# Values stationary and scaled probabilities moving for head pairs, in a two-block attention kernel

## The chip, the cores and the metric

One core of a Trainium2 chip runs the whole kernel. The metric is the device time of one execution in microseconds (us).

## The reference

Two transformer blocks work on one sequence of 256 tokens, width 1024, head width 64, all in f32. The first block has two layers; each runs four kinds of attention side by side (neighbourhood, differential, grouped-query, latent; 4 heads of each, the differential ones with two probability matrices). The second block has four layers: sliding-window, gated linear, forgetting, sliding-window. A feed-forward part follows every attention. Per head the attention is

```
p = softmax(q @ k.T * scale + table)      # 256 x 256, some heads causal, sliding heads with a sink in the sum
o = p @ v                                 # 256 x 64
```

and the heads side by side (256 x 1024) go through w_o.

## The kernel before

Weights come in units of 1 MB. ACT casts each to its leading part (`whi`, L885), DVE subtracts to get the rest (`wlo`, L894, sometimes in halves), and PE multiplies with three products of leading parts and rests. PE does a unit in four quarters.

A `Plan` says for each slot of a layer which quarters PE does, at which slot a head begins (`begin`), when a turn is made and which half units DVE splits. There are four plans: MIX (first block, 20 heads, of which 0 to 7 are the differential ones, called pair heads here, and 12 plain), SWA and FOX (sliding, forgetting, 16 plain causal heads each), and GLA (no heads of this kind). If head k begins in slot h, its steps are these.

- Slot h: PE computes the scores into a bank of `psu` (L751). DVE adds the table and finds the negated maximum (L846), or only the maximum (L840). ACT takes the exponential with its sums (L810, for a sink L808 before it) into `prob` and raises `p_ready`.
- Slot h+2: PE waits for `p_ready` and transposes `prob` into `pso` (L737), three 128x128 blocks for a causal head, four for another. ACT copies them to `probT` (L796).
- Slot h+3: PE multiplies `probT` (stationary, 128x128) by the values (64 columns moving) into `psm` (L766). DVE adds the sink to the sum (L819), takes the reciprocal (L821) and multiplies into `rows` (L828).
- "Turns": when the 128 columns m of the output (two heads) are in `rows`, PE transposes them into `psu` bank 1 (L612), ACT casts them to `ahi` (L645) and DVE subtracts to get `alo` (L649). These are the stationaries of w_o, whose quarters (the slab, L632) fill the last slots.

"Joint" pairs have both scores computed in one slot, side by side on the two halves of the partitions; the second head's go to bank 2 of `psy`, which the slab later takes, so that pairs are joint only up to the slot `pairs_to`.

Each engine runs its queue in order. In one slot DVE's is: maximum of the head that begins, division of the head three slots back, turn, rotary embedding (L1559 to L1563, SWA alone), half unit of `wlo`, and for two slots of the first SWA layer a modulation reduction (L1096). In a few slots the division comes first. ACT's is: copy of the transposed probabilities, exponential, casts of outputs, turn, `whi`.

## Time and profile before

| | |
|---|---|
| median of 3 runs | 1897.2 us (1896.7 to 1898.39) |
| profiled execution | 1897.12 us |
| its span | 1895.1 us |
| granted clock, mean | 0.998 |
| PE, DVE, ACT busy | 1855.8, 1354.9, 953.2 us |

The span runs from the first to the last instruction of the core. A timeline row starts with the start in us and the busy time in us. Matmuls overlap in the pipeline, so the pace of PE is read from start to start, not from busy times. L12 is line 12 of the kernel; names before the arrow are what is written. In brackets stands idle time ahead of the row and what ended it.

### The profile page before, as it was taken

The page shows a single profiled execution, that of the slowest core. Times are in us where ns is not written, and L with a number is a line of the kernel's source. Part 1 is how long each engine was busy: PE and PEld are TensorE (multiplying, and loading weights), DVE is VectorE, ACT ScalarE, POOL GpSimd, SP SyncE. Part 2 cuts the span into 40 slices and gives each one's busy share as a digit, 9 for nine tenths or more (in the row PEclk, how much of TensorE's full clock was granted, in tenths as well). Part 3 has the DMA queues.
Part 4 walks back from the last instruction along what each step waited for, and adds up shares of the span by engine and source line. Part 5 has one row for each costly group of instructions (what it writes and reads, how often), then busy time and mean ns, then how long its engine had stood idle before and what let it go on. Part 6 is the DMA issues. An engine that isn't in the chain of part 4 may idle for free.

```text
span 1895.1 us, 34211 instructions
## 1 busy us (share of the span) xinstructions
PE 1855.8 (98%) x13368; PEld 1702.6 (90%) x13368; DVE 1354.9 (71%) x2194; ACT 953.2 (50%) x1470; POOL 77.0 (4%) x98
## 2 busy tenths in 40 slices
PE   8999999999999999999999999999999999999998
PEld 8989999998999987899989799998989998979997
DVE  6758888775878877888877587886555556766555
ACT  7755334766533466533473553345654334664333
POOL 3003000000000000000000000003300000000000
PEclk9999999999999999999999999999999999999999
DMA  8538987533788742788854388875335554335552
GB/s 305 188 125 259 353 307 304 190 134 134 290 329 307 297 177 97 262 326 308 315 198 139 119 300 323 306 279 225 122 138 190 192 181 165 132 113 199 189 187 89
DMA packets 62060, 416.60 MB, mean 220 GB/s; under 512 B 9008, under 2 KB 9200, under 8 KB 13312
## 3 DMA queue, kind: packets, MB, share of 16 engines
q1 hardware_dynamic: 56016, 401.33, 57.4%
q0 software_dynamic: 5936, 13.79, 2.6%
q8 instruction: 72, 1.18, 0.2%
q14 instruction: 36, 0.29, 0.0%
HBM read 413.90 MB, written 3.19 MB: 220 GB/s over the span
## 4 chain that ended last, share of the span: by engine, by line
PE 89%; DVE 6%; ACT 2%; issue 1%; DVEq 1%; ACTq 0%; DMA 0%; SPq 0%
PE psu L524 35%; PE psy L692 18%; PE psy L586 7%; PE psy L578 5%; PE psy L632 5%; PE psu L541 4%; PE psm L766 3%; PE psy L565 2%; PE psu L751 2%; PE pso L737 1%; PE psy L655 1%; DVE x L1164 1%; DVE wlo L894 1%; PE psy L1680 1%; DVEq L1163 1%
## 5 line engine op out<-in xcount | busy, mean ns | idle before, releaser
L885 ACT CAST whi<-raw 128x2048 fp32r<-128x2048 f32 (+1 forms) x281 | 536.2, 1908 | 599.1 <-PE psu L524 396.4
L894 DVE TENSOR_TENSOR wlo<-raw,whi 128x2048 fp32r<-128x2048 f32 (+5 forms) x306 | 646.6, 2114 | 257.2 <-ACT whi L885 256.5
L524 PE MATMUL psu<-hlo,whi 128*128 128x256 f32 x1920 | 536.0, 279 | 0.0
L524 PE MATMUL psu<-hhi,whi 128*128 128x256 f32 x1920 | 535.9, 279 | 0.0
L524 PE MATMUL psu<-hhi,wlo 128*128 128x256 f32 x1920 | 535.8, 279 | 0.0
L524 PEld LDWEIGHTS psu<-hhi,whi 128*128 128x128 f32 x1920 | 360.8, 188 | 2.3
L524 PEld LDWEIGHTS psu<-hlo,whi 128*128 128x128 f32 x1920 | 360.8, 188 | 2.3
L524 PEld LDWEIGHTS psu<-hhi,wlo 128*128 128x128 f32 x1920 | 360.8, 188 | 0.0
L1096 DVE CUSTOM_DVE_ANT_0 ada_raw<-ada_raw,cvec 128x1024 f32<-128x1024 f32 x192 | 227.0, 1220 | 2.2 <-DMA ada_raw<-ada 2.2
L692 PE MATMUL psy<-whi,ahi 128*128 128x512 f32 x528 | 210.2, 398 | 0.0
L692 PE MATMUL psy<-wlo,ahi 128*128 128x512 f32 x528 | 207.9, 394 | 0.0
L692 PE MATMUL psy<-whi,alo 128*128 128x512 f32 x528 | 207.4, 393 | 0.0
L586 PE MATMUL psy<-whi,hhi 128*128 128x256 f32 x448 | 131.4, 293 | 0.0
L586 PE MATMUL psy<-wlo,hhi 128*128 128x256 f32 x448 | 125.9, 281 | 0.0
L586 PE MATMUL psy<-whi,hlo 128*128 128x256 f32 x448 | 125.8, 281 | 0.0
L692 PEld LDWEIGHTS psy<-wlo,ahi 128*128 128x128 f32 x528 | 99.1, 188 | 25.4
L692 PEld LDWEIGHTS psy<-whi,alo 128*128 128x128 f32 x528 | 99.1, 188 | 21.0
L692 PEld LDWEIGHTS psy<-whi,ahi 128*128 128x128 f32 x528 | 99.1, 188 | 20.5
L586 PEld LDWEIGHTS psy<-whi,hhi 128*128 128x128 f32 x448 | 84.5, 189 | 4.9 <-issue 4.8
L766 PEld LDWEIGHTS psm<-work 128*128 128x128 f32 x608 | 76.1, 191 | 13.5 <-issue 7.2
L810 ACT ACTIVATE work<-work,nmax 128x256 f32<-128x256 f32 (+1 forms) x144 | 66.5, 463 | 40.9 <-DVE nmax L846 40.9
L586 PEld LDWEIGHTS psy<-whi,hlo 128*128 128x128 f32 x448 | 84.6, 189 | 0.1
(337 smaller groups left out, 2981.2 us busy)
## 6 DMA issues: line engine op xcount, KB each, us to landing
raw<-wts SPq DMA_DIRECT2D x280, 1024.0 KB, 4.8
ada_raw<-ada SPq DMA_DIRECT2D x96, 1024.0 KB, 5.0
gain<-gate_rows POOLq DMA_DIRECT2D x8, 512.0 KB, 3.9
dense_bias<-rel_bias POOLq DMA_DIRECT2D x32, 64.0 KB, 10.1
nab<-dense_bias SPq DMA_DIRECT2D x2, 1024.0 KB, 7.1
ada_raw<-fox_rows POOLq DMA_DIRECT2D x4, 512.0 KB, 13.3
cb<-cst POOLq DMA_DIRECT2D x1, 1408.0 KB, 8.2
cb<-cst SPq DMA_DIRECT2D x1, 1056.0 KB, 10.1
```

What stands on the lines that cost most here:

```text
L524: last = mm(psu[:, bank, cc * SEQ:(cc + 1) * SEQ], a[:, cols], h[:, kt, :], start=(kt == 0 and j == 0), stop=(kt == KT - 1 and j == 2))
L541: last = mm(psu[:, banks[u], cc * SEQ:(cc + 1) * SEQ], a[:, cols], h[:, kt, :], start=(kt == 0 and cc == 0 and j == 0), stop=(kt == KT - 1 ...
L565: last = mm(psy[:, j, half * width:(half + 1) * width], h[:, kt, toks], a[:, kt * width:(kt + 1) * width], start=start, stop=stop, skip_gr ...
L578: last = mm(o, a[:, cols], h[:, kt, :], start=(kt == 0 and j == 0), stop=(kt == KT - 1 and j == 2))
L586: last = mm(o, h[:, kt, toks], a[:, kt * width:(kt + 1) * width], start=(kt == 0 and j == 0), stop=(kt == KT - 1 and j == 2))
L632: last = mm(psy[:, 2 * t + half, :], h[:, (2 * s + ff) % 4, toks], b[:, cols], start=(s == 0 and ff == 0 and j == 0), stop=(s == 3 and ff ...
L692: last = mm(psy[:, 2 * t + half, :], h[:, aslot + ff, toks], b[:, cols], start=(first_step and ff == 0 and j == 0), stop=(last_step and ff ...
L766: last = mm(psm[:, t * HD:(t + 1) * HD], probT[:, k % 2, at:at + P], it["v"][kc], start=(kc == 0), stop=(kc == 1 or at == P))
L810: last = nc.scalar.activation(prob[:, k % 2, span], src[:, span], ACT.Exp, bias=nmax[:, k % 4, t:t + 1], scale=1.0 if plain else -1.0, acc ...
L885: nc.scalar.copy(whi[:, part_of(c), 0:n], raw[:, slot_of(c), 0:n]).then_inc(hi_done, 1)
L894: last = nc.vector.tensor_tensor(wlo[:, part_of(c), cols], raw[:, slot_of(c), cols], whi[:, part_of(c), cols].bitcast(f32), ALU.subtract)
L1096: last = nc.vector.tensor_tensor_reduce(tile, tile, cvec[:], 1.0, 0.0, ALU.mult, ALU.add, ada_part[:, 2 * half + j:2 * half + j + 1])
```

## The change

1. For plain heads the product with the values is made for two heads at once, in the odd head's slot: values stationary (128x64), `probT` moving (256 columns, or 128 for the causal half), the even head into partitions 0 to 63 of `psm`, the odd one into 64 to 127. The output comes out transposed, and the PE turn falls away, but for the two of MIX that hold pair heads and the eight of GLA. ACT and DVE make `ahi` and `alo` from SBUF.
2. The normalisation goes ahead of the transposition: DVE's `dve_roots` (sink added, reciprocal) stands first in the slot after the scores, and waits for `p_ready`; ACT's `act_normal` scales `prob` in place before that slot's exponential. PE's transposition waits for it (`pn_ready`).
3. The division of two heads becomes one copy of 128x256 from `psm` (L865 of the changed kernel).
4. `probT` has three buffers, not two.
5. In SWA and FOX the second head's scores go to bank 1 of `psu`, which no turn uses now. `pairs_to` rises from 23 to 25 in FOX and from 16 to 20 in SWA: five more pairs are joint (two in each SWA layer, one in FOX). Two waits of the slab for `max_ready` go.

The diff, cut:

```diff
    [14, 16, 18, 20, 26, 27, 28, 30], "00 10 01 11 02 12 03 13",
-   [2, 3] + [2 * j + 1 for j in range(2, 11)] + [24, 25, 27, 29, 31, 33], 23)
+   [2, 3] + [2 * j + 1 for j in range(2, 11)] + [24, 25, 27, 29, 31, 33], 25)
 SWA = Plan([4] * 6, [2] * 8 + [1] * 15 + [2, 2, 1, 2, 2], range(6, 22), [11, 13, 15, 17, 20, 21, 23, 25],
-   "00 01 10 02 03 11 12 13", [2, 4, 6, 8, 13, 17, 20, 24], 16)
+   "00 01 10 02 03 11 12 13", [2, 4, 6, 8, 13, 17, 20, 24], 20)
 GLA = Plan([4] * 13, [3, 4, 1] + [1] * 60, [], [45, 46, 49, 50, 52, 53, 55, 57], "00 10 01 11 02 12 03 13",
...
-prob, probT = fold(w(8000, 1024), 2, 512), fold(w(9024, 1024), 2, 512)
+prob, probT = fold(w(8000, 1024), 2, 512), fold(w(9024, 1536), 3, 512)
...
-def act_turn(act, l, c, m, g, bank=1):
...
-    act.wait_ge(m_tr, 8 * g + m + 1)
+def act_turn(act, l, c, m, g, src, *ready):
+    act.wait_ge(*ready)
...
-    nc.scalar.copy(ahi[:, m % 4], psu[:, bank, 0:SEQ]).then_inc(m_hi, 1)
...
-def dve_turn(dve, m, g, bank=1):
+    nc.scalar.copy(ahi[:, m % 4], src).then_inc(m_hi, 1)
+def dve_turn(dve, m, g, src):
...
-    nc.vector.tensor_tensor(alo[:, m % 4], psu[:, bank, 0:SEQ], ahi[:, m % 4].bitcast(f32), ALU.subtract).then_inc(m_lo, 1)
+    nc.vector.tensor_tensor(alo[:, m % 4], src, ahi[:, m % 4].bitcast(f32), ALU.subtract).then_inc(m_lo, 1)
 def pe_norm(pe, m, q, idle=0, ahead=4):
...
 def score_at(plan, k):
-    return psy[:, 2] if plan.joint[k] and k % 2 == 1 else psu[:, 0]
+    second = psy[:, 2] if plan is MIX else psu[:, 1]
+    return second if plan.joint[k] and k % 2 == 1 else psu[:, 0]
 def spans(it):
...
+def turned_at(it, t, kc, at):
+    return at if it["causal"] or it["pair"] is not None else kc * SEQ + t * P
+def columns(plan, m):
+    at = 256 if plan is MIX and m == 4 else m * SEQ
+    return scratch[:, at:at + SEQ]
+def plain_no(I0, items, k):
+    before = sum(it["pair"] is None for it in items[:k])
+    return I0 - 8 * min(I0 // 20, DEPTH1) + before
 def pe_begin(pe, I0, items, plan, h):
...
-        pe.wait_ge(p_ready, I0 + k + 1)
+        if items[k]["pair"] is None:
+            pe.wait_ge(pn_ready, plain_no(I0, items, k) + 1)
+        else:
+            pe.wait_ge(p_ready, I0 + k + 1)
...
-        for _, _, at in blocks(items[k]):
-            last = nc.tensor.transpose(pso[:, at:at + P], prob[:, k % 2, at:at + P], ident[:])
+        for t, kc, at in blocks(items[k]):
+            to = turned_at(items[k], t, kc, at)
+            last = nc.tensor.transpose(pso[:, to:to + P], prob[:, k % 2, at:at + P], ident[:])
...
         it = items[k]
+        if it["pair"] is None and k % 2 == 0:
+            return
         pe.wait_ge(pt_ready, I0 + k + 1)
         if k >= 1:
-            pe.wait_ge(o_evac, I0 + k)
+            pe.wait_ge(o_evac, I0 + k - (it["pair"] is None))
         if it["vpre"] is not None:
             pe.wait_ge(*it["vpre"])
+        if it["pair"] is None:
+            for kc in range(2):
+                for i in (k - 1, k):
+                    toks, at = (slice(kc * P, SEQ), P + kc * SEQ) if it["causal"] else (slice(0, SEQ), kc * SEQ)
+                    last = mm(psm[HD * (i % 2):HD * (i % 2) + HD, toks], items[i]["v"][kc],
+                              probT[:, i % 3, at:at + toks.stop - toks.start], start=(kc == 0), stop=(kc == 1))
+            last.then_inc(o_done, 2)
+            return
         for t, kc, at in blocks(it):
-            last = mm(psm[:, t * HD:(t + 1) * HD], probT[:, k % 2, at:at + P],
+            last = mm(psm[:, t * HD:(t + 1) * HD], probT[:, k % 3, at:at + P],
                       it["v"][kc], start=(kc == 0), stop=(kc == 1 or at == P))
...
-def pe_mix_turn(pe, I0, plan, h, g):
...
-    m = plan.turn.get(h)
-    if m is not None:
-        pe.wait_ge(o_evac, I0 + 2 * m + 2)
-        pe_turn(pe, g, m)
...
 def pe_mix1_turn(pe, l, I0, h):
     m = MIX.turn.get(h)
-    if m is not None:
-        if m < 2:
-            pe.wait_ge(mix_ready, l + 1)
-        else:
-            pe.wait_ge(o_evac, I0 + 2 * m + 6)
+    if m is not None and m < 2:
+        pe.wait_ge(mix_ready, l + 1)
         pe_turn(pe, l, m)
 def act_copy(act, I0, items, plan, h):
...
         act.wait_ge(t_done, I0 + k + 1)
-        if k >= 2:
-            act.wait_ge(o_done, I0 + k - 1)
+        if k >= 3:
+            act.wait_ge(o_done, I0 + k - 2)
         lo = spans(items[k])[0].start
-        nc.scalar.copy(probT[:, k % 2, lo:], pso[:, lo:]).then_inc(pt_ready, 1)
+        nc.scalar.copy(probT[:, k % 3, lo:], pso[:, lo:]).then_inc(pt_ready, 1)
 def act_exp(act, I0, items, plan, h):
...
-def dve_divide(dve, I0, it, k):
+def act_normal(act, I0, items, plan, h):
+    k = plan.score(h - 1)
+    if k is not None and items[k]["pair"] is None:
+        act.wait_ge(r_ready, plain_no(I0, items, k) + 1)
+        for t, span in enumerate(spans(items[k])):
+            last = nc.scalar.activation(prob[:, k % 2, span], prob[:, k % 2, span], ACT.Copy, scale=rsum[:, k % 4, t:t + 1])
+        last.then_inc(pn_ready, 1)
+def dve_roots(dve, I0, items, plan, h):
+    k = plan.score(h - 1)
+    if k is not None and items[k]["pair"] is None:
+        dve.wait_ge(p_ready, I0 + k + 1)
+        if items[k]["sink"] is not None:
+            nc.vector.tensor_tensor(psum_[:, k % 4], psum_[:, k % 4], esink[:, k % 4], ALU.add)
+            nc.vector.drain()
+        nc.vector.reciprocal(rsum[:, k % 4], psum_[:, k % 4]).then_inc(r_ready, 1)
+def dve_divide(dve, I0, items, plan, k):
+    it = items[k]
+    if it["pair"] is None:
+        if k % 2 == 1:
+            dve.wait_ge(o_done, I0 + k + 1)
+            m = k // 2 - (2 if plan is MIX else 0)
+            nc.vector.tensor_copy(columns(plan, m), psm[:, 0:SEQ]).then_inc(o_evac, 2)
+        return
     dve.wait_ge(o_done, I0 + k + 1)
-    if it["sink"] is not None:
-        nc.vector.tensor_tensor(psum_[:, k % 4], psum_[:, k % 4], esink[:, k % 4], ALU.add)
-        nc.vector.drain()
     nc.vector.reciprocal(rsum[:, k % 4], psum_[:, k % 4])
...
 def dve_steps(dve, I0, items, plan, h, g, divide_first=False):
+    dve_roots(dve, I0, items, plan, h)
...
-        dve_divide(dve, I0, items[k], k)
+        dve_divide(dve, I0, items, plan, k)
...
     if k is not None and not divide_first:
-        dve_divide(dve, I0, items[k], k)
+        dve_divide(dve, I0, items, plan, k)
     if second is not None:
...
     if h in plan.turn:
-        dve_turn(dve, plan.turn[h], g)
+        m = plan.turn[h]
+        dve_turn(dve, m, g, psu[:, 1, 0:SEQ] if plan is MIX and m < 2 else columns(plan, m))
...
                     pe.wait_ge(swa_evac, s5 + (4 if part == 0 else 5))
-                    if part == 2:
-                        pe.wait_ge(max_ready, I0 + sum(SWA.joint))
                 pe_slab_quarter(pe, DEPTH1, c0 + 6, j - 6, part, g)
...
                     pe.wait_ge(bank_free, b0 + (12 if part == 0 else 13))
-                    if part == 0:
-                        pe.wait_ge(max_ready, I0 + sum(FOX.joint))
                 pe_slab_quarter(pe, DEPTH1, c0 + 13, j - 13, part, g, 1 if j == 13 else 0)
...
         pe_value(pe, I0, items, FOX, h)
-        pe_mix_turn(pe, I0, FOX, h, g)
         if h == 4:
...
+        act_normal(act, I0, items, SWA, h)
...
         if h in SWA.turn:
-            act_turn(act, DEPTH1, c0 + 6, SWA.turn[h], g)
+            m = SWA.turn[h]
+            act_turn(act, DEPTH1, c0 + 6, m, g, columns(SWA, m), o_evac, I0 + 2 * m + 2)
         if h == 23:
...
```

MIX and FOX take the lines of ACT like SWA. Three places follow where the instructions move. DVE, plain slots of an SWA layer; L846 before is L894 after, L894 before is L944 after, `psum_` the sums. Before:

```order
L846 ISA work,nmax<-psu,cb,nsink 128x128 [waits t_done,s_done]
L846 ISA nmax 128x1
L846 ISA work,nmax<-psu,cb,nsink 128x256
L846 ISA nmax 128x1
L819 TENSOR_TENSOR psum_<-psum_,esink 128x2 [waits o_done]
L821 RECIPROCAL rsum<-psum_ 128x2
L828 TENSOR_TENSOR rows<-psm,rsum 128x2x64
L894 TENSOR_TENSOR wlo<-raw,whi 128x1024 [waits hi_done]
```

After:

```order
L854 TENSOR_TENSOR psum_<-psum_,esink 128x2 [waits p_ready]
L856 RECIPROCAL rsum<-psum_ 128x2
L894 ISA work,nmax<-psu,cb,nsink 128x128 [waits t_done,s_done]
L894 ISA nmax 128x1
L894 ISA work,nmax<-psu,cb,nsink 128x256
L894 ISA nmax 128x1
L865 COPY rows<-psm 128x256 [waits o_done]
L944 TENSOR_TENSOR wlo<-raw,whi 128x1024 [waits hi_done]
L854 TENSOR_TENSOR psum_<-psum_,esink 128x2 [waits p_ready]
```

The sum and the reciprocal went from behind the maximum, where they waited for PE, to ahead of it, where they wait for ACT's exponential. ACT, the same layer, before:

```order
L796 COPY work<-pso 128x384 [waits o_done,t_done]
L808 ACTIVATE esink<-nmax,prow 128x2 [waits max_ready]
L810 ACTIVATE work,psum_<-work,nmax 128x128
L810 ACTIVATE work,psum_<-work,nmax 128x256
L645 CAST ahi<-psu 128x256 [waits m_tr]
```

After:

```order
L818 COPY work<-pso 128x384 [waits o_done,t_done]
L844 ACTIVATE work<-work,rsum 128x128 [waits r_ready]
L844 ACTIVATE work<-work,rsum 128x256
L830 ACTIVATE esink<-nmax,prow 128x2 [waits max_ready]
L832 ACTIVATE work,psum_<-work,nmax 128x128
L832 ACTIVATE work,psum_<-work,nmax 128x256
L647 CAST ahi<-rows 128x256 [waits o_evac]
```

Two scalings, with a wait for DVE, stand now between copy and exponential. PE, two slots of an SWA layer (an odd head with its turn), before:

```order
L751 MATMUL psu<-work 128x128 [waits swa_evac,max_ready]
L751 MATMUL psu<-work 128x256
L766 MATMUL psm<-work 128x64 [waits o_evac,pt_ready]
L766 MATMUL psm<-work 128x64 x2
L612 MATMUL psu<-ident,rows 128x128 [waits m_lo,o_evac]
L612 MATMUL psu<-ident,rows 128x128
```

After:

```order
L760 MATMUL pso<-ident,work 128x128 [waits pt_ready,pn_ready]
L760 MATMUL pso<-ident,work 128x128 x2
L774 MATMUL psu<-work 128x128 [waits swa_evac,max_ready]
L774 MATMUL psu<-work 128x128
L774 MATMUL psu<-work 128x256 x2
L794 MATMUL psm<-work 64x256 [waits o_evac,pt_ready]
L794 MATMUL psm<-work 64x256
L794 MATMUL psm<-work 64x128 x2
```

The value product is four instructions for two heads, the pair of scores is joint, and the turn is gone.

## Rows read from the trace of the kernel before

**Rows 1.** The page: busy time and instructions of each engine; its chain by engine.

```profile
PE 1855.8 (98%) x13368; PEld 1702.6 (90%) x13368; DVE 1354.9 (71%) x2194; ACT 953.2 (50%) x1470; POOL 77.0 (4%) x98
...
PE 89%; DVE 6%; ACT 2%; issue 1%; DVEq 1%; ACTq 0%; DMA 0%; SPq 0%
```

**Rows 2.** Windows: stretch, length, busy (instructions) of PE, PEld, DVE, ACT, POOL; clock, DMA.

```profile
712.00:726.00 14.00, 13.73 (x111) 12.05 (x110) 10.27 (x37) 9.65 (x32) 0.00 (x0) 1.00 0.05 7
1356.00:1372.00 16.00, 16.00 (x141) 15.50 (x141) 8.18 (x22) 9.76 (x22) 0.00 (x0) 1.00 0.39 133
116.00:132.00 16.00, 16.00 (x104) 14.09 (x104) 7.92 (x18) 9.78 (x24) 0.00 (x0) 1.00 0.34 133
```

**Rows 3.** Timeline of PE, sliding layer: start, busy, line, tiles, count.

```profile
704.52 0.78 PE L766 MATMUL psm<-work 128*128 128x64 f32 x6
705.11 0.36 PE L586 MATMUL psy<-whi,hhi 128*128 128x256 f32 x1
...
707.05 0.37 PE L751 MATMUL psu<-work 64*128 64x128 f32 x1
...
707.90 0.55 PE L766 MATMUL psm<-work 128*128 128x64 f32 x3
...
734.32 0.88 PE L766 MATMUL psm<-work 128*128 128x64 f32 x6
735.01 0.47 PE L632 MATMUL psy<-whi,ahi 128*128 128x512 f32 x1
```

**Rows 4.** Timeline of PE, first-block layer.

```profile
132.69 1.00 PE L766 MATMUL psm<-work 128*128 128x64 f32 x8
133.50 0.48 PE L632 MATMUL psy<-whi,ahi 128*128 128x512 f32 x1
133.82 0.40 PE L632 MATMUL psy<-whi,alo 128*128 128x512 f32 x1
134.06 0.39 PE L632 MATMUL psy<-wlo,ahi 128*128 128x512 f32 x1
...
136.39 0.38 PE L612 MATMUL psu<-ident,rows 128*128 128x128 f32 x2
136.53 0.48 PE L632 MATMUL psy<-whi,ahi 128*128 128x512 f32 x1
```

**Rows 5.** Timeline of PE, gated layer, a stationary of 64 columns.

```profile
1045.13 1.94 PE L1713 MATMUL psu<-work 128*64 128x256 f32 x8
```

**Rows 6.** Timeline of DVE, first sliding layer.

```profile
710.74 0.35 DVE L846 CUSTOM_DVE_ANT_0 work<-psy,cb,nsink 128x128 f32<-128x128 f32 x1 [1.15 <-PE pso L737]
...
711.42 0.16 DVE L819 TENSOR_TENSOR psum_<-psum_,esink 128x2 f32<-128x2 f32 x1
...
713.00 0.42 DVE L649 TENSOR_TENSOR alo<-psu,ahi 128x256 fp32r<-128x256 f32 x1 [0.82 <-ACT ahi L645]
...
715.64 0.15 DVE L819 TENSOR_TENSOR psum_<-psum_,esink 128x2 f32<-128x2 f32 x1
...
720.82 1.22 DVE L894 TENSOR_TENSOR wlo<-raw,whi 128x1024 fp32r<-128x1024 f32 x1
```

**Rows 7.** Timeline of ACT, first sliding layer.

```profile
711.54 0.29 ACT L808 ACTIVATE esink<-nmax,prow 128x2 f32<-128x2 f32 x1 [0.27 <-DVE nmax L846]
711.74 0.39 ACT L810 ACTIVATE work<-work,nmax 128x128 f32<-128x128 f32 x1
...
712.53 0.19 ACT L810 ACTIVATION_READ_ACCUMULATOR work<-work,nmax 128x1 f32 x1
712.62 0.35 ACT L645 CAST ahi<-psu 128x256 fp32r<-128x256 f32 x1
```

**Rows 8.** Timelines, PE of first, DVE and PE of second sliding layer.

```profile
750.62 0.49 PE L737 MATMUL pso<-ident,work 128*128 128x128 f32 x3
...
1644.14 0.35 DVE L846 CUSTOM_DVE_ANT_0 work<-psy,cb,nsink 128x128 f32<-128x128 f32 x1 [1.15 <-PE pso L737]
...
1682.97 0.49 PE L737 MATMUL pso<-ident,work 128*128 128x128 f32 x3
```

More of the change, by code:

```diff
@@ L260, in build @@
         o_evac = sem("o_evac")
+        r_ready = sem("r_ready")
+        pn_ready = sem("pn_ready")
         mix_ready = sem("mix_ready")
@@ L607, in pe_turn @@
         def pe_turn(pe, g, m, bank=1):
-            if not isinstance(m, int) or m > 0:
+            if m > 0:
                 pe.wait_ge(m_lo, 8 * g + m)
@@ L1329, in act_mix1 @@
                 act_copy(act, I0, items, MIX, h)
+                act_normal(act, I0, items, MIX, h)
                 act_exp(act, I0, items, MIX, h)
@@ L1374, in act_mix1 @@
                 if h in MIX.turn:
-                    act_turn(act, l, C1_O, MIX.turn[h], l)
+                    m = MIX.turn[h]
+                    if m < 2:
+                        act_turn(act, l, C1_O, m, l, psu[:, 1, 0:SEQ], m_tr, 2 * l + m + 1)
+                    else:
+                        act_turn(act, l, C1_O, m, l, columns(MIX, m), o_evac, I0 + 2 * m + 6)
                 if h == 33:
@@ L1599, in pe_swa @@
                     heads(SWA_HEADS[h])
-                pe_mix_turn(pe, I0, SWA, h, g)
         def pe_fox(pe, n, c0, b0):
@@ L1775, in act_fox @@
                 act_copy(act, I0, items, FOX, h)
+                act_normal(act, I0, items, FOX, h)
                 act_exp(act, I0, items, FOX, h)
@@ L1788, in act_fox @@
                 if h in FOX.turn:
-                    act_turn(act, DEPTH1, c0 + 13, FOX.turn[h], g)
+                    m = FOX.turn[h]
+                    act_turn(act, DEPTH1, c0 + 13, m, g, columns(FOX, m), o_evac, I0 + 2 * m + 2)
                 if h == 28:
@@ L1883, in act_gla @@
                 if h in GLA.turn:
-                    act_turn(act, DEPTH1, c0 + 13, GLA.turn[h], g, 0)
+                    act_turn(act, DEPTH1, c0 + 13, GLA.turn[h], g, psu[:, 0, 0:SEQ], m_tr, 2 * DEPTH1 + GLA.turn[h] + 1)
                 if h == 57:
@@ L1990, in dve_gla @@
                 if h in GLA.turn:
-                    dve_turn(dve, GLA.turn[h], g, 0)
+                    dve_turn(dve, GLA.turn[h], g, psu[:, 0, 0:SEQ])
                 if h in (4, 40):
```

## Prediction

> **What bounds the kernel now.** The first view is the page. PE is busy for 98% of the span and holds 89% of the chain; DVE holds 6%, ACT 2% [rows 1]. So what PE is spared shortens the kernel, as long as PE gets its inputs in time. Whether it does is not to be read from the means, so the second view is busy time by stretch [rows 2]. Among forgetting and first-block heads PE is busy for 16.00 of 16 us, with DVE at about 8 and ACT at 9.8: PE is the bound and the others have slack. Among sliding heads PE has 13.73 of 14 us, DVE 10.27, ACT 9.65. These heads have one quarter per slot, the ropes and the short slots, and the other engines wait for each other there. The third view is the timelines, for the prices and for the ring of waits between DVE and ACT.
>
> **PE, the part that is removed.** Heads of the sliding layer: six passes of a 64-column product take 704.52 to 705.11, 0.59 us; behind scores 734.32 to 735.01, 0.69 [rows 3]. Two heads: 1.28, and the change of format behind a product is paid once more (0.08: the first 512-column step behind it takes 133.50 to 133.82, 0.32, the next 0.24 [rows 4]). The new product of a pair has the passes of a joint pair of scores, two of 256 and two of 128 columns on each of two halves of the array. That pair takes 707.05 to 707.90, 0.85 [rows 3]. I take this for the values too: 1.36 - 0.85 = 0.51 saved per pair, 24 such pairs (16 sliding, 8 forgetting). A first-block head takes 132.69 to 133.50, 0.81 [rows 4], two of them with the change behind 1.70. The new pair has two passes of 256 where the causal pair has 128, so 0.85 + 2 x 0.12 = 1.09, with 0.24 per pass of 256 from 1.94 / 8 [rows 5]; 0.61 saved, 12 pairs.
>
> What no row shows is two *column* halves at once: rows 3 show two row halves of the array doing so. The bounds are 0.85 (they run side by side) and 0.85 + 0.72 = 1.57 (the second head's 256 + 256 + 128 + 128 columns behind the first's, three passes of 0.24, as the eight of rows 5 follow each other on one half). I take the lower end since the row that is nearest in form, two 64-wide tiles side by side, is the joint pair. The upper end is a rival. The Trainium skill, "TensorEngine Tiling (Array Packing)", Key Properties, says that tiles operate independently, but also "Mode switching requires drain". By its second rule each of the 36 products now drains the array twice, which the old ones with the whole array did not; the joint pair's 0.85, which begins with 128x128 transposes before it and a full-width product behind it, holds such a switch already, so the sum stays.
>
> Turns: 136.39 to 136.53, 0.14 [rows 4], and up to 0.22 with the step behind it; I take 0.18. There are eight turns in each of six layers; 12 of the 16 in MIX, 16 in SWA and 8 in FOX go, 36. Joint scores: a single head's scores take as long as a pair's, so 0.85 for each of five pairs. PE is spared 24 x 0.51 + 12 x 0.61 + 36 x 0.18 + 5 x 0.85 = 12.2 + 7.3 + 6.5 + 4.3 = **30.3 us**, if it never waits more.
>
> **DVE** loses the multiplication of each head (about 0.3) and gains a copy per pair (about 0.3): nothing to count. Its turn from SBUF is not dearer than the 0.42 us of now [rows 6].
>
> **ACT** gains two scalings for each of 72 heads. No row shows this; the nearest are the exponentials of the same blocks, 711.74 to 712.62, less two readings of the sum at 0.09 [rows 7]: 0.70 for a causal head, and with two of 256 columns 0.8. 48 x 0.70 + 24 x 0.8 = 53 us, of which nothing shows where ACT has its 6 us of slack in 16, as in the forgetting stretch.
>
> **The new ring.** Before, DVE could take the maximum of the next head while ACT was still at the exponential of this one. Now the sum and reciprocal stand ahead of that maximum and wait for the exponential. Everything DVE has queued ahead (turn, rope, half unit) then stands between this exponential and the next. One plain slot: roots 0.35; from the start of the maximum to ACT's start 710.74 to 711.54, 0.80; from there to the end of the exponential 1.08, and 0.12 for the signal (711.42 to 711.54). 2.35 us; the scaling (0.70) fits beside the 0.80. From the maximum of head 5 to that of head 15 in the first sliding layer: ten such, 23.5; five turns, each 713.00 - 711.54 + 0.42 - 1.20 = 0.68, 3.4; two ropes, each 715.64 - 713.00 - 0.42 = 2.2, 4.4; five half units at 1.22, 6.1; two modulation halves at 1.22, 2.4 [rows 6, 7]. Sum 39.8. To the transposition of head 15, which opens the rest of the slab: 0.80 + 1.20, a turn 0.68, a half 1.22, roots 0.35, scaling and signal 0.82, sum 5.1. So 44.9, where now 710.74 to 750.62 is 39.9 [rows 6, 8]: 5.0 later, less about 0.6 of product and turns that are cheaper behind it: **+4.4**. The second sliding layer has no modulation: 42.5, against 1644.14 to 1682.97, 38.8 [rows 8]: +3.7 - 0.6 = **+3.1**. PE's savings in front of the transposition are turned into waiting there.
>
> In the forgetting layer there is no rope, two quarters per slot keep PE at 16.00 of 16, and the ring has time: 8 x 0.51 + 8 x 0.18 + 0.85 = 6.4 saved, less 1 for the first heads, which wait behind a whole unit of DVE: **-5.4**. In the first block 6 x 0.61 + 6 x 0.18 = 4.8 per layer could be had. Some four heads begin in the 16 us, so ACT there goes from 9.8 to 9.8 + 4.2 x 0.8 = 13.2 [rows 2], and masks, turns and whole units of 2 us stand in DVE's queue ahead of roots. I give one third: **-1.6** per layer, between nothing and 4.8. Moving the banks of the scores takes no more than their waits; I cost it at nothing, as PE is behind its producers there.
>
> Sum: 4.4 + 3.1 - 5.4 - 3.2 = **-1.1 us**, from the profiled 1897.12 (the median is 1897.2, so it makes no difference): **1896.0 us**. A measurement of this kernel tells 0.2%, 3.8 us, from no change.
>
> **The rivals.**
>
> *A, the forecast: the ring bounds the sliding layers, tiles run side by side.* For it: the waits just worked out, and the 13.73 of 14. Against: my walk adds latencies in a row, and 1 us in ten slots on either side is easily missed. Own range 1889 to 1901. Chance 0.45.
>
> *B, column halves run one behind the other.* Place: the new product. Price: 0.72 more per causal pair, 0.96 per first-block pair. Against A: forgetting +5.8; first block: 6 x (0.96 - 0.61) - 6 x 0.18 = +1.0 and the delay of its first plain heads, 0.5, so 1.5 instead of -1.6, +6.2 for two layers; sliding +0.5 at most, as PE waits there. 1896.0 + 12.5 = 1908.5. It decides the sign from about 0.3 us more per pair. For it: every row with a 64-column stationary (rows 5) goes at one pass after the other. Against: the row halves do not. Chance 0.2. The Trainium skill, "TensorE: Matmul & The Clock Gate", Measured speedup vs the span model, gives 2.38x for three column tiles at once; by that page B falls, and no row of before shows it.
>
> *C, PE stays the bound everywhere.* DVE's and ACT's slack takes ring and scaling. 1897.1 - 30.3 = 1866.8; with the sliding ring as in A and the first block whole, 7.5 - 6.4 - 9.6 = -8.5, 1888.6. For it: the chain's 89% on PE. Against: ACT would have to do 0.70 more per slot of 3.6 us (39.9 / 11) in sliding layers and DVE never to stand behind it. Chance 0.25 for what lies from 1866 to 1889.
>
> *D, a dearer ring.* The half units that stand ahead of the roots themselves wait for ACT's cast to `whi`, which comes after its exponential, so that one late cast delays a whole slot. 2 us per layer more in three layers and the first block's third lost: 1896 + 6 + 3.2 = 1905. Chance 0.1.
>
> **How the numbers follow.** The time is A's. The range 1877 to 1909 takes in A, B and D and the dearer half of C; some 0.13 lies below, some 0.07 above. Faster by over 0.2% (under 1893.4): C with 0.25 and 0.12 of A, 0.37. Within: A's rest, 0.33, and 0.02 of D, 0.35. Slower: B and the rest of D, 0.28.
>
> **What would show it.** In the changed profile the value product should take 0.85 from start to start in sliding and 1.09 in first-block layers; 1.5 and more is B. The scaling should take 0.35 per instruction. In the sliding layers PE's transposition should wait for ACT's scaling, ACT for DVE's maximum, DVE's sum for ACT's exponential, and from the maximum of head 5 to the transposition of head 15 should be 45 us; with 40 or less A is wrong and C holds. In the forgetting layer PE should stay at 16 of 16. DVE's share of the chain should rise above its 6%. I would be most wrong if the transpositions of the first-block layers found the scaling ready each time.

## The result: 1908.1 us, 0.57% slower, and the profile after

| | before | after |
|---|---|---|
| median, 5 runs each | 1897.2 us (1896.7 to 1898.39) | 1908.1 us (1907.59 to 1909.43) |
| ratio | | 1.0057, 95% interval 1.0043 to 1.0072 |
| profiled execution, span | 1897.12, 1895.1 us | 1907.82, 1906.0 us |

Five runs of before, not three, stand behind 1897.2. The forecast was 1896.0, no change that could be told. The kernel is slower, clear of its interval; the time lies in the range of 1877 to 1909, near its upper end. The page after, against [rows 1]:

```profile
PE 1836.4 (96%) x13104; PEld 1658.1 (87%) x13104; DVE 1345.6 (71%) x2158; ACT 1005.9 (53%) x1614; POOL 78.1 (4%) x98
...
PE 84%; DVE 7%; ACT 5%; issue 2%; DVEq 2%; ACTq 1%; DMA 0%; SPq 0%
```

PE is busy 19.4 us less and holds 84% of the chain instead of 89%, and the kernel is 11 us longer. ACT is busy 52.7 us more; 53 was worked out. DVE and ACT have gained chain. The same three stretches of time as in [rows 2]; the work in them has moved by 2 to 11 us, so they show how full each engine is and not the same instructions:

```profile
712.00:726.00 14.00, 12.52 (x102) 10.00 (x101) 8.74 (x34) 12.31 (x38) 0.00 (x0) 1.00 0.21 75
1356.00:1372.00 16.00, 15.95 (x135) 14.01 (x135) 7.91 (x26) 13.12 (x33) 0.00 (x0) 1.00 0.38 132
116.00:132.00 16.00, 14.46 (x77) 10.31 (x76) 7.16 (x15) 11.65 (x31) 0.00 (x0) 1.00 0.23 78
```

The forgetting stretch is still full, 15.95 of 16. In the sliding and first-block stretches PE now stands still for 1.5 us each. In the sliding one ACT is nearly as busy as PE, 12.31 of 14.

**Where the time went, layer by layer.** The last matmul of the w_o slab marks the end of each layer's attention. Its start (L632 before, L634 after), less that of before, less what had been gained or lost by the layer ahead, gives each layer's own part. The first sliding layer, for example: 763.69 before, 775.47 after, 11.78 late, of which 6.56 came from the layers ahead; 5.22 is its own. A layer's own part also holds the feed-forward part ahead of its attention; that matters for the two kernels with POOL's reciprocal, as told there. The table has the runs of the next section too; figures in us, negative is faster than before.

```
                 first 1  first 2  sliding  gated  forgetting  sliding 2
the change         2.33     4.23     5.22   -0.06     -5.06      4.34
no_scaling        -3.11    -3.05    -2.87    0.18     -4.99     -4.12
free_scaling      -1.01    -1.86    -0.39    0.02     -5.01     -1.65
thin_scaling       0.33     0.85     3.82    0.16     -5.23      2.71
pool_roots        -0.28    -1.89     4.65   -1.08     -6.12      5.58
dve_scaling        0.96     1.28    11.74    0.35     -3.14     10.00
roots_late         7.02     8.50    11.62    0.03     -4.44     10.33
normal_late        9.93    10.72    16.72   -0.05     -1.33     17.03
both_late         10.11    10.52    15.23    0.00     -1.38     15.10
few_joint          2.56     4.24     6.36    0.00     -4.10      4.15
fox_only           0.09     0.08    -0.12    0.03     -4.71     -0.19
mix_fox_pool      -0.43    -2.21    -1.06   -0.52     -6.09      0.20
fill_after         2.56     2.77     5.36   -0.02     -4.65      4.33
```

**The value product.** Timelines of PE after, a sliding, a first-block and a later sliding layer:

```profile
714.71 0.87 PE L794 MATMUL psm<-work 128*64 128x256 f32 x8
715.51 0.38 PE L588 MATMUL psy<-whi,hhi 128*128 128x256 f32 x1
...
107.41 1.08 PE L794 MATMUL psm<-work 128*64 128x256 f32 x8
108.43 0.50 PE L634 MATMUL psy<-whi,ahi 128*128 128x512 f32 x1
...
752.96 1.55 PE L794 MATMUL psm<-work 128*64 128x256 f32 x8
754.43 0.65 PE L634 MATMUL psy<-whi,ahi 128*128 128x512 f32 x1
```

From start to start 0.80 and 1.02 us, where [rows 3] had 0.59 and 0.69 per head and [rows 4] 0.81. The two column halves run side by side; one behind the other they would take 1.5 and more by the prediction's sum. The third took 1.47 at a granted clock of 0.5, half of full speed, which is close to twice the 0.80. More on that below.

**First block.** The timelines of DVE, ACT and PE after, at the first plain heads of the first layer (ACT L844 is the scaling, DVE L856 the reciprocal, L1146 the modulation):

```profile
86.00 1.22 DVE L1146 CUSTOM_DVE_ANT_0 ada_raw<-ada_raw,cvec 128x1024 f32<-128x1024 f32 x1
...
87.41 0.16 DVE L856 RECIPROCAL rsum<-psum_ 128x2 f32<-128x2 f32 x1
...
94.50 0.69 DVE L1520 TENSOR_REDUCE gs<-work 128x8 f32<-128x512 f32 x1
95.11 0.15 DVE L856 RECIPROCAL rsum<-psum_ 128x2 f32<-128x2 f32 x1
97.61 0.69 DVE L1524 TENSOR_TENSOR rows<-rows,gs 128x512 f32<-128x512 f32 x1 [2.35 <-ACT gs L1424]
98.98 2.28 DVE L944 TENSOR_TENSOR wlo<-raw,whi 128x2048 fp32r<-128x2048 f32 x1
101.18 0.16 DVE L856 RECIPROCAL rsum<-psum_ 128x2 f32<-128x2 f32 x1
```

```profile
87.60 0.91 ACT L844 ACTIVATE work<-work,rsum 128x256 f32<-128x256 f32 x2 [1.54 <-DVE rsum L856]
...
95.30 0.91 ACT L844 ACTIVATE work<-work,rsum 128x256 f32<-128x256 f32 x2 [1.13 <-DVE rsum L856]
96.11 0.45 ACT L832 ACTIVATE work<-psy,nmax 128x256 f32<-128x256 f32 x1
...
97.36 0.21 ACT L1424 ACTIVATE gs<-gs 128x8 f32<-128x8 f32 x1
...
101.37 0.91 ACT L844 ACTIVATE work<-work,rsum 128x256 f32<-128x256 f32 x2 [3.33 <-DVE rsum L856]
```

Read them from the top. The reciprocal of head 8 stands behind the modulation until 87.41, ACT stands 1.54 us for it, and what is behind the scaling in ACT's queue waits too: an exponential that had its maximum long ago. The reciprocal of head 10 stands behind sums of the differential heads until 95.11. The exponential behind its scaling starts at 96.11; before, the same one started at 92.79. DVE then needs a square root that ACT computes behind it (97.36), waits 2.35 us, and its whole unit starts at 98.98 instead of 95.94. The reciprocal of head 11 is behind that unit, at 101.18. PE's transposition of head 11 went from 98.61 to 102.34. Before, that exponential waited for no reciprocal, and DVE stood 0.21 us for the same root. A wait of 1 us went round between the two queues, and each time picked up what stood in the way.

**Sliding layers.** The chain of waits after, for two slots (start, us, what; L854, L856 sum and reciprocal, L832 exponential, L651 turn):

```profile
727.26 0.88 ACT work L832 x4
728.14 0.30 ACT ahi L647
728.46 0.42 DVE alo L651
728.89 1.14 DVEq L855
730.02 0.07 DVE psum_ L854
...
730.17 0.18 DVE rsum L856
730.34 0.02 issue
730.37 0.77 ACT work L844 x2
...
731.31 0.97 ACT work L832 x4
```

This is the ring: exponential, turn, half unit (here as DVE's queue, 1.14), sum and reciprocal, scaling, next exponential. In these two slots PE is not in it. Its length, from the maximum of head 5 to the transposition of head 15, from the timelines after:

```profile
717.67 0.35 DVE L894 CUSTOM_DVE_ANT_0 work<-psu,cb,nsink 128x128 f32<-128x128 f32 x1 [0.45 <-PE pso L760]
...
758.06 0.35 DVE L894 CUSTOM_DVE_ANT_0 work<-psu,cb,nsink 128x128 f32<-128x128 f32 x1
```

```profile
763.11 0.33 PE L760 MATMUL pso<-ident,work 128*128 128x128 f32 x1 [1.20 <-ACT work L844]
```

40.4 and 5.1 us, 45.4 in all; 39.8, 5.1 and 44.9 were forecast. The sum came out, its pieces only in part. From one maximum to the next the two slots with turn and rope took 5.90 and 5.69 us, where 5.23 was worked out, and a slot with a half unit alone 2.52 for 3.57:

```profile
730.31 0.35 DVE L894 CUSTOM_DVE_ANT_0 work<-psu,cb,nsink 128x128 f32<-128x128 f32 x1
...
732.83 0.35 DVE L894 CUSTOM_DVE_ANT_0 work<-psu,cb,nsink 128x128 f32<-128x128 f32 x1
```

DVE does such a half unit while ACT is at the exponential, so it costs the ring next to nothing. The slot with a half unit and the modulation took 4.81 for 6.01. The last two together took 8.08 for 6.60; there ACT casts a whole unit (751.86, 1.88 us) ahead of a scaling and an exponential. What was taken too dear, 2.4 us, and what was taken too cheap, 2.9, nearly cancel. Over the whole kernel, the groups of PE's transposition and of ACT's scaling after:

```profile
L760 PE MATMUL pso<-ident,work 128*128 128x128 f32 x304 | 49.7, 280 | 27.0 <-ACT work L844 27.0
```

```profile
L844 ACT ACTIVATE work<-work,rsum 128x256 f32<-128x256 f32 (+1 forms) x144 | 60.4, 468 | 44.4 <-DVE rsum L856 43.9
```

PE waits 27.0 us for the scaling (0.1 ahead of its transpositions before), ACT 43.9 us for the reciprocal.

### The profile page after: what moved, and what is told of

It reads as the page before. It is cut to its first block, busy times and chain, and to the rows that moved or that the text cites. A ratio compares the mean times of both kernels' runs of the same rounds, so it can differ in the third digit from the quotient of the medians.

```text
span 1906.0 us, 33678 instructions
## 1 busy us (share of the span) xinstructions
PE 1836.4 (96%) x13104; PEld 1658.1 (87%) x13104; DVE 1345.6 (71%) x2158; ACT 1005.9 (53%) x1614; POOL 78.1 (4%) x98
## 4 chain that ended last, share of the span: by engine, by line
PE 84%; DVE 7%; ACT 5%; issue 2%; DVEq 2%; ACTq 1%; DMA 0%; SPq 0%
PE psu L526 35%; PE psy L694 18%; PE psy L588 6%; PE psy L580 5%; PE psy L634 4%; PE psu L543 4%; PE psy L567 2%; ACT work L832 2%; PE psu L774 2%; PE psy L657 1%; ACT work L844 1%; DVE wlo L944 1%; DVE x L1214 1%; PE pso L760 1%; PE psm L794 1%
## 5 line engine op out<-in xcount | busy, mean ns | idle before, releaser
L944 DVE TENSOR_TENSOR wlo<-raw,whi 128x2048 fp32r<-128x2048 f32 (+5 forms) x306 | 645.5, 2111 | 255.5 <-ACT whi L935 254.7
L1146 DVE CUSTOM_DVE_ANT_0 ada_raw<-ada_raw,cvec 128x1024 f32<-128x1024 f32 x192 | 226.9, 1219 | 2.5 <-DMA ada_raw<-ada 2.5
L694 PE MATMUL psy<-whi,ahi 128*128 128x512 f32 x528 | 210.2, 398 | 0.0
L634 PE MATMUL psy<-whi,ahi 128*128 128x512 f32 x192 | 82.1, 428 | 2.8 <-ACT work L1791 2.1
L588 PEld LDWEIGHTS psy<-wlo,hhi 128*128 128x128 f32 x448 | 84.4, 188 | 0.0
```

The lines of the kernel that those rows point to most:

```text
L588: last = mm(o, h[:, kt, toks], a[:, kt * width:(kt + 1) * width], start=(kt == 0 and j == 0), stop=(kt == KT - 1 and j == 2))
L634: last = mm(psy[:, 2 * t + half, :], h[:, (2 * s + ff) % 4, toks], b[:, cols], start=(s == 0 and ff == 0 and j == 0), stop=(s == 3 and ff ...
L694: last = mm(psy[:, 2 * t + half, :], h[:, aslot + ff, toks], b[:, cols], start=(first_step and ff == 0 and j == 0), stop=(last_step and ff ...
L944: last = nc.vector.tensor_tensor(wlo[:, part_of(c), cols], raw[:, slot_of(c), cols], whi[:, part_of(c), cols].bitcast(f32), ALU.subtract)
L1146: last = nc.vector.tensor_tensor_reduce(tile, tile, cvec[:], 1.0, 0.0, ALU.mult, ALU.add, ada_part[:, 2 * half + j:2 * half + j + 1])
```

## The experiments

**Moving the two new steps back in their queues** was the first idea: if they stand in the way, let them stand behind.

```diff
 # normal_late: in act_mix1, act_swa, act_fox
-act_normal(act, I0, items, SWA, h)
 act_exp(act, I0, items, SWA, h)
+act_normal(act, I0, items, SWA, h)
 # roots_late: in dve_steps; both_late has both
-dve_roots(dve, I0, items, plan, h)
 k = plan.value(h)
...
         second = k + 1 if pair else None
+dve_roots(dve, I0, items, plan, h)
```

> The changed kernel with ACT's scaling moved behind the exponential of its slot, in all three plans. Theory Q (queues): the loss is two waits set ahead of work that doesn't need them; the exponential stands behind a scaling that waits for DVE's reciprocal, which stands behind DVE's other work. Without the first of them the 1.5, 1.1 and 3.3 us that ACT stands in the first-block layer fall away, and each first-block layer goes from 2.3 and 4.2 us slower than before to 2 faster: 1908 - 10 = 1898. The sliding layers keep the other wait and gain 1 us or less each. Theory V (volume): the 53 us of scaling are too much for ACT, wherever they stand: 1906 to 1909.

> The changed kernel with DVE's sum and reciprocal moved behind the (first) maximum of the slot. Theory Q: the maximum no longer waits for the exponential of the head before, but the scaling, and so the exponential, waits longer for the reciprocal. The sliding layers gain 1 to 3 us each, the first-block layers gain nothing or lose 1: 1902 to 1908. Theory V: no change, 1908.

> Both moves at once: sum and reciprocal behind the maximum, scaling behind the exponential. Theory Q: maximum and exponential run as before, the ring is gone, and PE's spared work shows: first-block layers 3 us faster than before each, forgetting layer 5 to 6, sliding layers 3 to 5 each: 1897 - 18 = 1879, at most 1888. Theory V: 1904 or more.

Measured: 1952.7, 1931.2 and 1944.57 us, ratios 1.029 (1.0276 to 1.0304), 1.0177 (1.0164 to 1.0191) and 1.0246 (1.0232 to 1.026). Theory Q missed by 23 to 57 us, with the wrong sign each time. Theory V missed the first two by over 20 us; the third it takes in only because "1904 or more" has no upper end. The groups of PE's transposition, roots_late first, normal_late second:

```profile
L760 PE MATMUL pso<-ident,work 128*128 128x128 f32 x304 | 51.7, 288 | 37.7 <-ACT work L844 37.6
```

```profile
L760 PE MATMUL pso<-ident,work 128*128 128x128 f32 x304 | 51.2, 285 | 63.9 <-ACT work L844 63.4
```

What happens is seen in the timeline of ACT in normal_late:

```profile
720.12 0.30 ACT L830 ACTIVATE esink<-nmax,prow 128x2 f32<-128x2 f32 x1 [2.01 <-DVE nmax L894]
720.32 0.39 ACT L832 ACTIVATE work<-work,nmax 128x128 f32<-128x128 f32 x1
...
721.20 0.79 ACT L844 ACTIVATE work<-work,rsum 128x128 f32<-128x128 f32 x2
```

The reciprocal for this scaling was done at 719.42 (DVE, 719.25 and 0.17), and ACT stood from 718.1 to 720.12 for the maximum of the next head. The scaling of head k-1 is wanted by PE at the next slot. Behind the exponential of head k it also waits for the scores of head k, which PE computes in this slot. So PE waits for something that waits for PE: scores, maximum, exponential, scaling, all in one slot. Ahead of the exponential it needs nothing from the slot. In roots_late the same loop closes through DVE, whose reciprocal now stands behind a maximum that waits for PE's scores of the slot (DVE, then ACT):

```profile
725.33 0.35 DVE L894 CUSTOM_DVE_ANT_0 work<-psu,cb,nsink 128x128 f32<-128x128 f32 x1 [1.20 <-PE psu L774]
...
726.44 0.80 ACT L844 ACTIVATE work<-work,rsum 128x128 f32<-128x128 f32 x2 [1.18 <-DVE rsum L856]
```

A part of what the three lose is the clock: its mean in their profiles is 0.991, in the change's 0.996. In 1930 to 1950 us that is 10 us at the most, of 23 to 45 us against the change. The change's order is the best of the four; the wait in it is the price of this.

**One layer kind alone.** The plans of first block and sliding layers as before; only the forgetting layer has the new scheme.

```diff
+NEW = (FOX, )
...
-                if items[k]["pair"] is None:
+                if scaled(plan, items[k]):
                     pe.wait_ge(pn_ready, plain_no(I0, items, k) + 1)
```

> The change in the forgetting layer alone; the other plans as before (probT with three buffers for all). Both theories: the forgetting layer is 5.1 us faster as in the changed kernel, the rest as before: 1892. If it is not, the layers depend on each other, and reading the loss layer by layer is wrong.

Measured: 1892.41 us, 0.9974 (0.9964 to 0.9985). The layer gains 4.71, the others are within 0.2 of before, as forecast. The loss can be read layer by layer, and three buffers of `probT` by themselves change nothing.

**What the wait costs and what the work costs.** Two kernels leave the normalisation of plain heads out: no_scaling has neither reciprocal nor scaling; free_scaling has the scaling instructions with a factor of one and neither reciprocal nor wait for it. thin_scaling has the wait, and scales one column only.

```diff
 # no_scaling
-act_normal(act, I0, items, SWA, h)
-dve_roots(dve, I0, items, plan, h)
-pe.wait_ge(pn_ready, plain_no(I0, items, k) + 1)
+pe.wait_ge(p_ready, I0 + k + 1)
 # free_scaling
-dve_roots(dve, I0, items, plan, h)
-act.wait_ge(r_ready, plain_no(I0, items, k) + 1)
+act.wait_ge(p_ready, I0 + k + 1)
...
-... ACT.Copy, scale=rsum[:, k % 4, t:t + 1])
+... ACT.Copy, scale=1.0)
 # thin_scaling
+span = slice(span.start, span.start + 1)
```

> The changed kernel without the normalisation of plain heads: no sum and reciprocal on DVE, no scaling on ACT, PE transposes after p_ready as before; value product, copy per pair, absent turns and joint pairs stay. This is what PE's part is worth by itself. If the value pass of 0.80 and 1.02 and the prices of turns and scores add up, 30 us faster than before: 1867 to 1872. If other waits hold PE then, 1875 or more.

> The changed kernel with ACT's scaling instructions in full, but by one, and no sum, reciprocal or wait for DVE: the volume alone. With no_scaling at 1869 as the one end and the change at 1908 as the other: theory R (the wait for DVE's reciprocal in ACT's queue, and the maximum behind it) puts it near the first, 1870 to 1885; theory V (volume of 53 us on ACT) near the other, 1890 to 1905.

> The changed kernel with each scaling on one column only, so that the probabilities stay unnormalised: ACT's two instructions and all waits stay, their length goes from about 0.46 busy to some 0.2. Theory V: the loss was this work, 144 x 0.25 = 36 us of ACT; the time falls by 10 us or more, under 1898. Theory R: ACT still waits for the reciprocal, and only the part of the scaling in the ring is saved (some 0.5 us per head where the ring bounds): 1901 to 1906.

| kernel | us | ratio to before | against the one above |
|---|---|---|---|
| before | 1897.1 | | |
| no_scaling | 1879.6 | 0.991 (0.9895 to 0.9925) | PE's part, with DVE rid of the roots: -17.5 |
| free_scaling | 1888.82 | 0.9954 (0.9941 to 0.9968) | scaling work on ACT: +9.2 |
| the change | 1908.1 | 1.0057 (1.0043 to 1.0072) | reciprocal and the waits with it: +19.3 |

So the change is a gain of at most 17.5 us by PE's part, with 28.5 us paid for it. Two thirds of these are for the reciprocal and two waits that come with it: ACT's scaling waits for DVE's reciprocal, and DVE's reciprocal, ahead of the maximum, waits for ACT's exponential. free_scaling takes both away and does not part them. The 17.5 are not PE's alone either: no_scaling also spares DVE the sum and reciprocal that before has (0.32 us of work per sliding head). Even so they fall short of the 30 forecast. In no_scaling PE stands 4.9 us for `alo` ahead of the turns that are left (0.7 before), 3.1 ahead of the slab for ACT's copies of the sliding layers' inputs, 2.3 ahead of transpositions for ACT's copy out of `pso` and 2.1 ahead of scores for a maximum (little or nothing of these before): some 11 us more of waiting. free_scaling landed between the two theories. So did thin_scaling, 1900.77 us (1.0017, 1.0008 to 1.0026): with all waits and 26 us less of ACT (34.7 instead of 60.4 busy) it gives back 7.3, where theory R had 2 to 7 and theory V 10 or more. Both theories hold a part, R the larger. In the forgetting layer all of these stand at -5: two quarters per slot hide work and wait.

**Another engine.** dve_scaling lets DVE multiply right behind its reciprocal; pool_roots has POOL add the sink and take the reciprocal in first-block and sliding layers.

```diff
 # dve_scaling, in dve_roots
+nc.vector.drain()
+for t, span in enumerate(spans(items[k])):
+    last = nc.vector.tensor_scalar(prob[:, k % 2, span], prob[:, k % 2, span], rsum[:, k % 4, t:t + 1], None, ALU.mult)
+last.then_inc(pn_ready, 1)
 # pool_roots, in POOL's queue, for the plain heads of a layer
+pool.wait_ge(p_ready, I0 + k + 1)
+if it["sink"] is not None:
+    nc.gpsimd.tensor_tensor(psum_[:, k % 4], psum_[:, k % 4], esink[:, k % 4], ALU.add)
+    nc.gpsimd.drain()
+nc.gpsimd.tensor_tensor(rsum[:, k % 4], psum_[:, k % 4], minus[:], ALU.pow).then_inc(r_ready, 1)
```

> The changed kernel with the scaling of prob on DVE, right behind its reciprocal (two tensor_scalar instructions per head), and none on ACT. Theory R: ACT's exponential no longer waits for the reciprocal, which gives back 4 to 6 us in each first-block layer; but DVE's maximum now waits for exponential, reciprocal and scaling, 0.65 us more per slot of the ring, so that the sliding layers lose 2 to 5 more each: 1900 to 1908. Theory V: ACT is relieved of 53 us, under 1895.

> The changed kernel, but in first-block and sliding layers POOL adds the sink and takes the reciprocal (as a power of -1), in its own queue, where it is idle; DVE does so in the forgetting layer only. Theory R (the reciprocal stands in DVE's queue: ACT's scaling waits for it 44 us in all, and DVE's maximum waits for the exponential): both waits go, the losses of 2.3 and 4.2 us in the first-block layers and 5.2 and 4.3 in the sliding ones turn into gains of 1 to 4 each: 1880 to 1890, if POOL takes under 1 us for the two small operations. Theory V (volume of the scaling on ACT): 1905 or more. Theory L (the chain exponential, reciprocal, scaling, transposition is too long by itself for slots of one quarter): 1900 to 1910.

dve_scaling: 1918.94 us, 1.0116 (1.0101 to 1.0132), outside both theories. In the first block it is 1.4 and 3.0 us better than the change, in the sliding layers 6.5 and 5.7 worse: the directions of theory R, but less given back and more lost than it had. pool_roots: 1896.32 us, 0.9995 (0.9986 to 1.0004), between theory R (1890 at most) and the two others (1900 or more). In the first block 2.6 and 6.1 better than the change, in the first sliding layer 0.6 better, in the second 1.2 worse. The group of the power on POOL in pool_roots, and POOL's timeline in a sliding layer:

```profile
L2064 POOL TENSOR_TENSOR rsum<-psum_,minus 128x2 f32<-128x2 f32 x56 | 44.8, 800 | 169.4 <-ACT work L762 162.4 <-issue 2.9
```

```profile
720.73 0.19 POOL L2062 TENSOR_TENSOR psum_<-psum_,esink 128x2 f32<-128x2 f32 x1 [1.98 <-ACT work L762]
721.06 0.89 POOL L2064 TENSOR_TENSOR rsum<-psum_,minus 128x2 f32<-128x2 f32 x1
```

Sum and power take 1.2 us on POOL, as long as the half unit that DVE's reciprocal waited behind. In the first block, where it stood behind 2.3 us and more, and a square root on ACT hung on it, POOL wins.

**A gain that is not the reciprocal's.** Part of this kernel's time has another source. Two casts of ACT at the ends of the feed-forward part behind the gated layer, where no edit changes anything, before and in mix_fox_pool, the kernel of the last experiment, which also has POOL's reciprocal:

```profile
1109.31 1.91 ACT L885 CAST whi<-raw 128x2048 fp32r<-128x2048 f32 x1
...
1277.03 1.91 ACT L885 CAST whi<-raw 128x2048 fp32r<-128x2048 f32 x1 [1.96 <-PE psy L692]
```

```profile
1105.15 1.91 ACT L889 CAST whi<-raw 128x2048 fp32r<-128x2048 f32 x1
...
1272.11 1.92 ACT L889 CAST whi<-raw 128x2048 fp32r<-128x2048 f32 x1 [1.86 <-PE psy L625]
```

167.72 us before, 166.96 there. In pool_roots and mix_fox_pool the dense products in front of the first attention and in the six feed-forward parts take 4.6 and 4.8 us less in all, up to 0.95 each; in the other kernels with the new scheme each feed-forward part is within 0.2 of before. What brings this is not known: what the two share beside the new scheme is POOL's program and one small buffer more. So of the 11.8 us that pool_roots is ahead of the change, 4.6 are not the reciprocal's. Taken out of the layers, POOL is about 2.5 and 5.6 us better in the first block, and 0.2 and 2.2 worse in the sliding layers.

**Joint pairs.** `pairs_to` back to 23 and 16.

> The changed kernel with the joint pairs of before (pairs_to 23 and 16). If PE were the bound in the sliding layers it would lose 5 x 0.85 = 4.3 us: 1912.4. By theory R the sliding layers wait elsewhere and only the forgetting layer pays its 0.85, and a single head's scores may even come sooner: 1907 to 1910.

1909.67 us, 1.0067 (1.0053 to 1.008), within the forecast: 1.6 more than the change, though the intervals of the two ratios overlap. By layers 1.0 of it is in the forgetting layer; the first sliding layer loses 1.1, the second gains 0.2.

**The clock.** Windows of the change, second first-block and first sliding layer; the column behind POOL's is the granted clock:

```profile
436.00:442.00 6.00, 4.87 (x17) 3.57 (x18) 2.87 (x10) 5.80 (x14) 0.00 (x0) 0.72 0.38 161
750.00:756.00 6.00, 5.11 (x25) 3.35 (x26) 2.26 (x12) 5.96 (x17) 0.00 (x0) 0.72 0.26 105
```

In both stretches the clock drops from 2.4 to 1.2 GHz for a few us. PE had stood 1.24 us ahead of the transposition at 435.34 and 1.13 ahead of a turn at 437.13, and 2.86 us ahead of the transposition at 750.89. The value product at 752.96 paid with 1.47 for 0.80. To see what this is worth, PE got products of zeros in the waits ahead of four transpositions:

```diff
+FILL = {MIX: {8: 3, 10: 4, 11: 4}, SWA: {12: 9}}
...
+                if k in FILL.get(plan, {}):
+                    pe.wait_ge(pt_ready, I0 + k)
+                    for _ in range(FILL[plan][k]):
+                        mm(fold(pso[:, 0:512], 4, P), zeros[:], zeros[:].unsqueeze(1).to_broadcast([P, 4, P]), start=True, stop=True)
```

> The changed kernel with products of zeros on PE (0.27 us each) in the waits ahead of the transpositions of heads 8, 10 and 11 of the first-block layers (three, four, four) and of head 12 of the sliding layers (nine). In the change's trace the granted clock is 0.5 from 437 to 441 and from 751 to 755 us, right behind such waits, and before's is 1.00 there. Theory K (part of the loss is the clock that falls behind the waits, up to 1.7 us for each of the two stretches): the stretches stay at 1.00 and the time falls by 1 to 4 us, 1904 to 1907; second first-block layer 4.2 to about 2.5, first sliding layer 5.2 to 4.3. Without it: 1908 to 1911, since a filler may also delay a transposition.

1907.07 us, 1.0048 (1.0034 to 1.0061). The same windows in fill_after:

```profile
436.00:442.00 6.00, 4.87 (x28) 3.20 (x27) 3.65 (x15) 5.80 (x15) 0.00 (x0) 1.00 0.38 157
750.00:756.00 6.00, 5.43 (x34) 3.39 (x31) 2.49 (x9) 5.34 (x15) 0.00 (x0) 1.00 0.07 26
```

The second first-block layer goes from 4.23 to 2.77, next to the first one's 2.56: the clock was worth 1.5 us there, and is the reason why the two equal layers differed. In the sliding layer the drop only moved to 758, behind a wait of 2.15 us, and nothing is gained. In the change the drop from 751 to 755 is not seen to cost: ACT goes without a wait from 750.04 to 756.2, and the chain of waits runs through it. The total is 1.0 better, and the intervals of the two ratios overlap, so the gain is shown by the layer alone. But the mean clock of the profile is back at 0.998, as before, from 0.996, and 1907.07 us remain: the clock is a small part of the loss.

**Both kernels beaten.** The new scheme where it pays: forgetting layer as in the change, first block with POOL's reciprocal, sliding layers as before.

> The change in first-block and forgetting layers, with POOL's reciprocal in the first-block ones; sliding layers as before. By the layers of the runs so far, -0.3 and -1.9 in the first-block layers, -4.8 in the forgetting one: 1897.2 - 7.0 = 1890.2, faster than fox_only's 1892.4. If the layers depend on each other, 1892 or more.

1886.17 us, 0.9941 (0.9927 to 0.9954): 11 us faster than before, 22 faster than the change, and 4 better than the sum forecast. But 4.8 of the 11 are the faster dense products told of above, so the scheme itself brings some 6. Without them the first block is at -0.2 and -1.3, forgetting at -5.3, the first sliding and the gated layer, which have the instructions of before, at -0.3 and +0.2, and the second sliding layer at +1.0; this last one stays unexplained.

## Why the prediction was wrong

It was wrong by 12.1 us, and most of it is one step, the first block.

- *Value product.* 0.80 and 1.02 against 0.85 and 1.09. Right, at the lower bound that was taken. Rival B gave 1908.5, within 0.4 us of the result, by a mechanism that did not take place; the time alone would have confirmed it, and the two rows refute it.
- *Forgetting layer.* -5.06 against -5.4. Right.
- *Sliding layers.* +5.2 and +4.3 against +4.4 and +3.1. The ring was there and as long as worked out, 45.4 us against 44.9, 43.2 against 42.5 in the second layer. That it is so close is in part luck: pieces 2.4 us too dear and 2.9 too cheap cancel in the first. Also, ACT was to wait for the maximum (0.80 in the sum). It waits for the reciprocal and then scales (0.77), which costs the same. The 0.8 and 1.2 us that these layers lost beyond the forecast are in about equal parts a ring that is longer and the 0.6 for cheaper product and turns behind it, which hardly showed.
- *First block.* +2.3 and +4.2 against -1.6 each. This step failed: "I give one third". The text named what stands ahead of the roots (masks, turns and whole units of 2 us) and did not walk it. I had counted what the scaling costs in ACT's time, 13.2 of 16 us, and concluded that part of the gain is left. What counted was which wait the scaling carries into ACT's queue. The modulation is the first of it, 1.54 us of standing, and the exponentials behind it were needed by DVE itself. 9.8 of the 12.1 us are here. That the wait is the cause is shown by pool_roots, in which the reciprocal stands behind no other work: about -0.1 and -1.3 there, with the faster dense products taken out. Its second layer also kept its clock, which fill_after puts at 1.5 of the 5.6 us.
- *ACT.* 0.81 for two scalings of 256 columns, 52.7 us in all against 53. Right. The price "of which nothing shows" in the forgetting layer was right; in the first block the work alone costs 2.1 and 1.2 us (free_scaling less no_scaling), in the sliding layers 2.5 each.
- *PE's 30.3 us.* With nothing in the way 17.5 were had. The sum counts each saving at full value; where other waits hold PE, a part of each is not there to be had. For the first block "4.8 per layer could be had" was too much by itself: 3.1 and 3.05 are had in no_scaling.
- *Clock.* No term of the sum was for it. It cost 1.5 us in one layer; in the first sliding layer no cost of it is seen.

Rival D (a dearer ring, 1905, 0.10) had the sign, but not the mechanism: none of DVE's half units from 717 to 763 us waits for ACT's cast. No rival had the reciprocal's wait that goes round in the first block.

## What to carry to other kernels

Before a step is put ahead in an engine's queue, ask what it waits for, what stands in front of that on the other engine, and who stands behind the step without needing it, and walk this through the slots in which the other engine has its long pieces, since means of busy time don't show it. Work taken from the busiest engine is worth its full length only if nothing else holds that engine then; one run with the new side work left out tells how much is to be had. Where layers differ in slack, turn a change on by layer. And where a variant comes out faster than its parts explain, look at a stretch that it does not touch.

## What the runs showed of the hardware

- Products with 64-column stationaries for the two halves of the output partitions overlap: two heads with 384 columns each took 0.80 us, less than the 0.85 of the joint scores with as many.
- Products of zeros, 0.27 us each, in waits of 1.2 us kept the clock at 1.00 where it had dropped to 0.5.
- POOL takes 0.80 us for a power of 128x2 elements, where DVE's reciprocal of the same takes 0.17 and its sum 0.16.
